# Block 2's first mixer as one stream of steps, with the softmax weights applied by ScalarE

## The reference, cut to what matters

```python
qa, ka, va, qb, kb, vb = jnp.split(hh @ w_in, EVEN_SPLITS, axis=-1)   # 8+2+2 and 8+8+8 heads of 64
qa = rms_norm(qa, a_qn); ka = rms_norm(ka, a_kn); qb = rms_norm(qb, b_qn); kb = rms_norm(kb, b_kn)
qa = rope_2d(qa, row, col); ka = rope_2d(ka, row, col)                 # latents only
# a: 4 query heads share a key head; |q - k| <= 128 among latents, all context keys, and a sink
p = softmax(concatenate([s_loc, s_ctx, s_sink], -1));  o_a = p[..., :nloc] @ vb + p[..., nloc:] @ vc
# b: neighbourhood with a position bias among latents, all context keys, no sink
s_loc = qg @ kg * scale + bias;  s_loc = where(col_ok, s_loc, NEG_INF)
y_lat = concatenate([o_a, o_b], -1) @ w_out                            # y_ctx the same, keys: context only
x = x + g1 * y_lat;  ctx = ctx + cg1 * y_ctx
```

## Time and profile before

| | us |
|---|---|
| Median of 3 timed runs (2628.22 to 2632.52) | 2629.16 |
| The profiled execution's own time | 2625.06 |
| Its span in the profile | 2623.4 |
| TensorE busy | 2340.9 (89%) |
| VectorE busy | 1578.5 (60%) |
| ScalarE busy | 830.6 (32%) |
| Projection of the mixer, from 1273.57 to 1381.10 | 107.53 |
| Head norms, rotation, bias, to 1440.38 | 59.28 |
| Attention, to 1593.50 | 153.12 |
| Output projection, to the first sum of the next norm at 1642.80 | 49.30 |

### The profile page before, as it was taken

The page is one execution under the profiler, slowest core; times in us unless marked ns, Lnnn a source line. Parts: engine busy times, 40 slices in busy tenths (PEclk is TensorE's granted clock), DMA queues, the critical chain, the costliest instruction groups (busy, mean ns, idle before and its releaser), DMA issues.

```text
span 2623.4 us, 39655 instructions
## 1 busy us (share of the span) xinstructions
PE 2340.9 (89%) x14932; PEld 1943.1 (74%) x14932; DVE 1578.5 (60%) x2834; ACT 830.6 (32%) x1274; POOL 29.0 (1%) x58
## 2 busy tenths in 40 slices
PE   8999579999999888999696999599999568797999
PEld 7999448999999877998582557478878453166987
DVE  6666667666666657665535884662552565556764
ACT  4444324444444544443010452011111010153332
POOL 0000000000000000000000000000000000000000
PEclk9999859999999988999896899799999787599999
DMA  7656204665665423666120002022222110001444
GB/s 249 240 208 218 81 0 154 238 213 199 241 230 184 154 97 125 237 221 236 68 96 0 1 1 85 32 96 96 96 96 96 48 65 16 0 1 65 160 169 151
DMA packets 50221, 325.66 MB, mean 124 GB/s; under 512 B 5328, under 2 KB 8656, under 8 KB 16976
## 3 DMA queue, kind: packets, MB, share of 16 engines
q1 hardware_dynamic: 42480, 266.61, 28.9%
q0 software_dynamic: 7648, 57.81, 6.0%
HBM read 323.35 MB, written 1.05 MB: 124 GB/s over the span
## 4 chain that ended last, share of the span: by engine, by line
PE 80%; DVE 14%; ACT 3%; issue 2%; DMA 0%; DVEq 0%; ACTq 0%; PEldq 0%; SPq 0%
PE psum L1319 17%; PE psum L1320 16%; PE psum L1321 16%; PE psum L1406 3%; PE psum L1444 3%; PE psum L1473 3%; PE psum L1407 3%; PE psum L1408 3%; PE psum L1491 3%; PE psum L1465 3%; PE psum L1701 2%; PE psum L1423 2%; PE psum L1480 1%; DVE w_lo L627 1%; PE psum L1702 1%
## 5 line engine op out<-in xcount | busy, mean ns | idle before, releaser
L1319 PE MATMUL psum<-h_hi,w_hi 128*128 128x256 f32 (+2 forms) x2568 | 796.7, 310 | 115.9 <-DVE h_lo L815 84.7
L393 ACT ACTIVATE w_hi<-raw 128x1024 fp32r<-128x1024 f32 (+1 forms) x542 | 513.6, 990 | 859.1 <-PE psum L1321 648.8
L1320 PE MATMUL psum<-h_lo,w_hi 128*128 128x256 f32 (+2 forms) x2568 | 785.1, 306 | 0.0
L1321 PE MATMUL psum<-h_hi,w_lo 128*128 128x256 f32 (+2 forms) x2568 | 784.6, 306 | 0.0
L627 DVE TENSOR_TENSOR w_lo<-raw,w_hi 128x1024 fp32r<-128x1024 f32 (+1 forms) x542 | 599.8, 1148 | 230.9 <-ACT w_hi L393 211.1
L1319 PEld LDWEIGHTS psum<-h_hi,w_hi 128*128 128x128 f32 (+1 forms) x2568 | 496.2, 193 | 162.7 <-issue 64.8
L1321 PEld LDWEIGHTS psum<-h_hi,w_lo 128*128 128x128 f32 (+1 forms) x2568 | 495.9, 193 | 19.4
L1320 PEld LDWEIGHTS psum<-h_lo,w_hi 128*128 128x128 f32 (+1 forms) x2568 | 496.1, 193 | 18.9
L1406 PE MATMUL psum<-g_both,w_hi 128*128 128x256 f32 x704 | 202.4, 287 | 2.1 <-DVE w_lo L627 2.1
L1407 PE MATMUL psum<-g_both,w_hi 128*128 128x256 f32 x704 | 199.1, 283 | 0.0
L1408 PE MATMUL psum<-g_both,w_lo 128*128 128x256 f32 x704 | 199.1, 283 | 0.0
(11 more groups left out here) (231 smaller groups left out, 2888.6 us busy)
## 6 DMA issues: line engine op xcount, KB each, us to landing
raw<-in_weights SPq DMA_DIRECT2D x207, 1024.0 KB, 4.9
raw_ada<-in_ada POOLq DMA_DIRECT2D x48, 1024.0 KB, 6.8
raw<-in_weights SPq DMA_DIRECT2D x64, 704.0 KB, 4.1
arena<-in_rpb POOLq DMA_DIRECT2D x1, 2048.0 KB, 9.7
arena<-in_fox_c POOLq DMA_DIRECT2D x1, 1888.0 KB, 8.7
const_region<-in_even_c POOLq DMA_DIRECT2D x1, 1360.0 KB, 8.8
const_region<-in_latent_c POOLq DMA_DIRECT2D x1, 1296.0 KB, 6.2
x_res<-in_x_lat SPq DMA_DIRECT2D x4, 256.0 KB, 6.9
```

The costliest lines, as they stand in the source:

```text
L393: nc.scalar.activation(wh[s][:, a], raw[s][:, a], ACT.Copy).then_inc(hi_ready, 1)
L1319: mm(out, sh, mh, start=n == 0, stop=False)
L1320: mm(out, sh, ml, start=False, stop=False)
L1321: ins = mm(out, sl, mh, start=False, stop=n == len(pairs) - 1)
```

## The change

Stages 1 to 4 become one list of things to do, `even_order`, which all engines follow. Its items are: a projection unit; the sum of one chunk's squares; a root over the 10 rows of the "a" heads or the 16 rows of the "b" heads; the spread of a chunk; the rotation of a chunk; a "slot" of attention; half an output unit.

The attention's 64 jobs are grouped in 24 steps (`even_steps`): for each kind and each of 4 chunks two wide steps (two heads, one block of 128 queries, 512 keys) and one narrow step (two heads, both query blocks, 256 keys). A slot k has, on TensorE, the scores of step k, the transposes of step k-1 and the value products of step k-2. The two heads of a step lie on partitions 0 to 63 and 64 to 127. Scores of every step use banks 2 and 3, transposes 4 and 5. Slots 0 to 11 (kind a) stand behind projection units 8 to 17 (two slots behind units 12 and 16), slots 12 to 26 behind the projection. Behind slots 15 to 22 stands one half output unit each (12 products, "a" half), and the 8 "b" halves come last.

Other edits: TensorE adds bias and mask as a product with the identity (line 1831 of the kernel after), the factor 1/8 is folded into the query gains, VectorE's maximum takes both heads in one instruction, and the weighting of the exponentials goes from VectorE to ScalarE (a copy with a scale). Squares go from VectorE to ScalarE. The mask is added to the bias by GpSimd in 2 instructions. The key copies go away, since heads c and c+4 form a pair (weights are permuted on the host). In `stick`, the choice of the table set moves behind the square root.

```diff
+            for n in range(18):
+                yield "unit", n
+                if 1 <= n <= 5 or 7 <= n <= 14:
+                    yield "sum", n - 1 - (n > 6)
...
+                if n >= 8:
+                    for _ in range(1 + (n in (12, 16))):
+                        yield "slot", next(slots)
+            for k in slots:
+                yield "slot", k
+                if 15 <= k <= 22:
+                    yield "out", k - 15
+            for q in range(8, 16):
+                yield "out", q
...
+            def step_slot(k):      # ScalarE
+                if k < len(E_STEPS):
+                    s, z = E_STEPS[k], 8 + 4 * (k % 2)
+                    nj = len(s["jobs"])
+                    act.wait_ge(st_shifted, k + 1)
+                    if s["kind"] == "a":
+                        nc.scalar.activation(st_small[:, 32 + z:32 + z + nj], st_small[:, 24 + z:24 + z + nj], ACT.Exp)
+                    for n, (m, t, col) in enumerate(s["jobs"]):
+                        nc.scalar.activation(st_p[:, 2 * (k % 2) + m, col:col + s["L"]], psum[:, 2 + m, col:col + s["L"]],
+                                             ACT.Exp, bias=st_small[:, z + n:z + n + 1],
+                                             accum_out=st_small[:, 8 + z + n:9 + z + n]).then_inc(st_exp, 1)
+                if 1 <= k <= len(E_STEPS):
+                    s, z = E_STEPS[k - 1], 24 + 4 * ((k - 1) % 2)
+                    act.wait_ge(st_rec, k)
+                    for n, (m, t, col) in enumerate(s["jobs"]):
+                        p = st_p[:, 2 * ((k - 1) % 2) + m, col:col + s["L"]]
+                        ins = nc.scalar.activation(p, p, ACT.Copy, scale=st_small[:, z + n:z + n + 1])
+                    ins.then_inc(st_prob, 1)
+                    act.wait_ge(st_turned, k)
+                    wait(act, st_out, k - 2)
+                    for m in range(2):
+                        nc.scalar.activation(st_pt[:, 2 * ((k - 1) % 2) + m, :], psum[:, 4 + m, :],
+                                             ACT.Copy).then_inc(st_turn_in, 1)
...
-                    nc.scalar.preload_act_table_set("natural_log_exp_and_others")
                     for what, k in stick_order():
                         if what == "proj":
                             stage(1, 1, 1, 1, lead=(lambda: square_one(7)) if k == (0, 0) else None)
+                            if k == (0, 0):
+                                nc.scalar.preload_act_table_set("natural_log_exp_and_others")
...
+            def step_shift(k):     # VectorE
+                dve.wait_ge(st_scored, k + 1)
+                ...
+                    step(V.reduce_max(mx, src, AX_X))
+            def step_weigh(k):
+                dve.wait_ge(st_exp, sum(len(v["jobs"]) for v in E_STEPS[0:k + 1]))
+                if s["kind"] == "a":
+                    step(V.tensor_tensor(tot, tot, es, ALU.add))
+                V.reciprocal(rec, tot).then_inc(st_rec, 1)
...
+            def step_scores(k):    # TensorE
+                wait(pe, st_exp, sum(len(v["jobs"]) for v in E_STEPS[0:k]))
+                ...
+                        ins = mm(psum[:, 2 + m, 0:T], ident, bias, start=False, stop=True)
+                ins.then_inc(st_scored, 1)
+            def step_turn(k):
+                pe.wait_ge(st_prob, k + 1)
+                wait(pe, st_turn_in, 2 * k)
...
+            def step_out(k):
+                pe.wait_ge(st_turn_in, 2 * k + 2)
...
+                    elif what == "slot":
+                        if k < len(E_STEPS):
+                            step_scores(k)
+                        if 1 <= k <= len(E_STEPS):
+                            step_turn(k - 1)
+                        if 2 <= k <= len(E_STEPS) + 1:
+                            step_out(k - 2)
```

More of the change, by code:

```diff
@@ new lines, in even_steps @@
+        def even_steps():
+            steps = []
+            for kind in "ab":
+                for c in range(4):
+                    group = 8 * (kind == "b") + 2 * c
+                    for t in range(2):
+                        steps.append(dict(kind=kind, c=c, base=0, L=TJ, jobs=[(m, t, 0) for m in range(2)],
+                                          group=group, first=t == 0, last=t == 1))
+                    steps.append(dict(kind=kind, c=c, base=T, L=T, jobs=[(m, t, t * T) for m in range(2) for t in range(2)],
+                                      group=group + 1, first=True, last=True))
+            return steps
@@ new lines, in even @@
+            def even():
+                sums = 0
+                unit_of = {}
+                for what, k in even_order():
+                    if what == "unit":
+                        if k % 2 == 0:
+                            hi_next(0, 0, 1, pos.e, SLOT)
+                            pos.p += 1
+                        unit_of[k] = pos.u
+                        pos.u += 1
+                        pos.e += 1
+                    elif what == "sum":
+                        act.wait_ge(bank_free, unit_of[k + (k >= 5)] + 3)
+                        wait(act, e_sq_used, sums - 1)
+                        nc.scalar.activation(e_sq[:, sums % 2, :], e_qk[:, k, :], ACT.Square).then_inc(e_sq_made, 1)
+                        sums += 1
+                    elif what == "root":
+                        rows = (10, 16)[k]
+                        act.wait_ge(e_sq_used, (5, 13)[k])
+                        nc.scalar.activation(e_row[0:rows, :], psum[0:rows, 7, :], ACT.Sqrt,
+                                             bias=small[0:rows, 40:41]).then_inc(e_rooted, 1)
+                    elif what in ("spread", "rope"):
+                        pos.u += 1
+                        pos.e += 1
+                    elif what == "slot":
+                        step_slot(k)
+                    else:
+                        if k % 4 == 0:
+                            hi_next(0, 0, 1, pos.e, SLOT)
+                            pos.p += 1
+                        pos.u += 1
+                        pos.e += 1
@@ L562, in _ @@
             norm(TJ)
-            for j in range(9):
-                stage(1, 1, 2, 2)
-            ask(ACT.Sqrt, row_t[0:26, :], row_t[0:26, :])
-            softmax_jobs(list(even_jobs()))
-            stage(2, 2, 2, 4)
+            even()
             norm(TJ)
@@ L1662, in even @@
-                pe.wait_ge(phase_loaded[2], 32)
-                head_norms([(P, TJ)] * 13, 26, TJ, lambda c: e_sel[:, c, 0:26], lambda c, m: e_bsel[0:26, c, :])
-                told()
-                for c in range(5):
-                    b = small_out()
-                    mm(psum[:, b, 0:T], rot_a[:], e_qk[:, c, 0:T], start=True, stop=True).then_inc(small_done, 1)
-                told()
-                softmax_jobs(list(even_jobs()))
-                stage(2, 2, 2, 4, lambda i, j, s: joint_chunks(i, j, s, 2))
+                sums, unit_of = 0, {}
@@ L1946, in _arrays @@
     out["sb_c"] = _join(np.concatenate([m0, m1], axis=1), tri, -np.ones((P, P)))
-    sel, bsel = _head_tables(13, 32)
+    sel, bsel = np.zeros((P, 13, 32), np.float32), np.zeros((32, 13, P), np.float32)
+    for first, n in ((0, 5), (5, 8)):
+        sel[:, first:first + n], bsel[:, first:first + n] = _head_tables(n, 32)
     cos, sin, rot = _rope(P, 16)
```

309 lines of the change are left out of this document (223 added, 86 removed).

## The result

The changed kernel takes 2691.84 us (median of 4 runs, 2688.99 to 2692.62) against 2629.32 for the kernel before (4 runs, 2628.22 to 2632.52): 1.0233 times as long, 95% interval 1.0218 to 1.0248. The forecast was 2702, from a chain of two claims: a stall in every slot, and a clock that falls behind each stall. Both are there.

The account below looks back on a forecast made before the run. TensorE, busy 89% of the span, was taken to bound the kernel: 2625.06 + 24 (mixer at full clock) + 69 (clock) - 20 (`stick`) = 2698, plus 4.1 from profiled execution to median, 2702 us; range 2635 to 2755.

Parts of the forecast that it names:

- Table loads of `stick`: In `stick`, table loads between exponentials and logarithms go: a gain of 20 us, ends 10 and 30.
- TensorE's work in the slots, full clock: In the attention, a pair of heads costs what one head costs: 91 us for what takes 153.12.
- Stall in 24 slots: In every slot, TensorE's transposes wait for ScalarE's weighting, queued behind the next exponentials: 112 us, ends 96 and 127.
- Clock loss in the slots: Behind each of 24 stalls, TensorE's clock falls and loses 2.65 us: 64 us.
- First five spreads, the unit ahead of them left out: In the mixer's norms, the first 5 spreads are not hidden: 5.4 us more than unit 6 itself.
- Mixer in all: The whole changed mixer, 369.2 us before, would be about 440 to 480 us long.
- GpSimd beside VectorE in the norm: In the norm ahead of the mixer, GpSimd's bias and mask addition beside VectorE costs 0 to 4 us, taken as 0.
- Rival 4: In the attention, pairs do not run at once with 512 keys: 41 us on top, 2743 us; chance 0.04.
- the second reciprocal: In the mixer's norms, it stands in front of VectorE's maximum: 2.1 us.
- Rival 1: In the slots, TensorE keeps its clock through the stalls: 69 us go, 2633 us, or 2609 at best; chance 0.13.
- Rival 2: In slots 12 to 26, without full units, the clock stays down: 116 us instead of 69, 2749 us; chance 0.20.
- rival 3: In the slots, transposes find their weights ready: 112 us and most clock loss go, about 2525 us; chance 0.03.

Follow-up runs that it names:

- e6: Kernel before, with only the choice of ScalarE's table set in `stick` moved behind the square root: 2604.77 us, 0.9907 of before.
- e5: Changed kernel with 5 unneeded 512-column products on TensorE between scores and transposes of every slot: 2648.81 us.
- e4: Changed kernel with GpSimd's two additions of mask to bias made to wait for the mixer's first squares: 2687.76 us.
- e3: Changed kernel with 7 unneeded 512-column products on TensorE between scores and transposes of every slot: 2674.04 us.
- e1: Changed kernel with ScalarE's weighting of step k, and VectorE's reciprocal for it, moved from slot k+1 to slot k: 2566.58 us, 0.9764 of before.
- e8: Changed kernel with weighting and reciprocal of step k in slot k, and the weighting on VectorE: 2553.21 us, 0.9717 of before.
- e9: e8 with GpSimd's additions waiting for first squares, VectorE's group reading earlier, second root and reciprocal behind the slot after unit 14: 2550.28 us, 0.9696 of before.
- e7: Changed kernel with the weighting of the exponentials back on VectorE instead of ScalarE, orders else kept: 2650.81 us.

## Why the prediction was right, and where it was off

| Term | forecast | shown |
|---|---|---|
| Table loads of `stick` | -20 | -22.5 in the profiles, -24.3 in e6 |
| TensorE's work in the slots, full clock | 91 | 91.7 (e5: 42.6 + 24.3 + 24.8) |
| Stall in 24 slots | 112 | 110.4: 109.5 in 23 slots, 0.85 in the last |
| Clock loss in the slots | 64 | 51 (e5 against the changed kernel) |
| First five spreads, the unit ahead of them left out | 5.4 | 7.2 (1306.42 to 1313.62) |
| Mixer in all | 462.5 | 449.6 |
| GpSimd beside VectorE in the norm | 0 | +4.4, 4.1 in e4 |
| Same work behind the mixer | 0 | +4.4, from execution to execution |

**The table loads.** Right in size and reason; e6 isolates it. The reason is mainly, but not only, the waits: the two that I had added up to 23.8 us fell to 7.5, and the clock gave about 4 us. By count 17 loads went and none came (23 from 800 us to the norm before, 6 now), where I had one put in.

**Work in the attention.** Right: pairs at once, also with 512 keys. Rival 4 (pairs apart) falls by the row at 1595.61, where four instructions for two heads take 1.06 us.

**The stall.** The deciding step, and right in place, releaser and total. Some of the agreement is luck, since misses cancel. The last stall is 0.85 us, because no scores and exponentials stand ahead of it, and I had counted it at 4.5; the other 23 are 4.76 us on average. The longest, 6.35, holds the second reciprocal, which I had as 2.1 us in a term of its own. And I took 1.15 us for weighting two times 512 and 1.4 for four times 256, and the rows at 720 and 500 ns make it 1.33 to 1.35 and 1.7. Other parts were shorter than I had allowed (the two exponentials 1.34 us from 1599.37 to 1600.71, where I had 1.44), so that the mean of all 24 is 4.60 us where I had 4.67. The trace of before held no such row, and the upper bound (the exponential's 0.72) was the better choice: the copy with its scale took 720 ns, the plain copy out of PSUM 595 (line 581). Both the exponential and this copy read a value per row; no run isolates what that costs.

**The clock.** Right in kind: idle time ahead of the transposes brings it to half, e3 and e5 show it by filling the idle time and changing nothing else. The size was the term most off, 64 for 51, and this is nearly the whole of the 12.9 us by which the mixer was too long in my sum. I had carried one wait's 2.65 us over to all 24. In the changed kernel transposes and values at half clock lose 0.9 + 0.9, and the half unit behind 0.4 to 0.7 (1606.26 to 1609.58 is 3.32 us, the same in e5 2.96), and some steps lost less. Rival 1 (clock holds) falls with PEclk 0.74 to 0.81. Rival 2 (stays down for long, 116 us) falls too: behind each of the eight half output units the scores run at full clock again (1.13 to 1.14 us in the timeline, from 1568.63 to 1664.14), though no full unit stands there. Its case in slots without a unit ahead is seen in part: scores and bias at 1495.42, 1523.44 and 1534.84 take 1.1, 0.8 and 0.2 us more than at full clock.

**The stall hidden** (rival 3, 2525 us). Not in this change, but e1, e8 and e9 are that case, built on purpose: 2567, 2553 and 2550. They stay 42, 28 and 25 us above it, since the 112 us did not all go: in e1 28 us of waits are left, and in e8 20.

**GpSimd.** This step failed: bounded by 0 and 4 and taken at 0, it is 4.4 in the profile, above the bound, and 4.1 in the time. I had looked at where GpSimd's result is needed, and not at what runs on VectorE beside it.

The profiled execution was put at 2698 and is 2691.5: -12.9 for the mixer and -2.5 for `stick`, +4.4 for GpSimd and +4.4 behind the mixer. I had added 4.1 for the distance of the median from the profiled execution before; the changed kernel's median and profiled execution agree within 0.4 us, so that distance belonged to one execution and should not have been carried over.

## What to carry to other kernels

When a pipeline over three engines is given a new order, write out for each engine what stands in front of the instruction for which another engine waits; here work on ready data (the weighting of step k-1) stood behind work on data not yet made (the exponentials of step k), and that cost 110 us of waits and 51 of clock, while the choice of engine cost 13 once the order was mended. Take a composite change apart: one of its edits was worth -24 us. And a wait that is found last in a ring is not the ring: removing its 14 us lowered all waits by 5, and the clock took 4 of these back.

## What the runs showed of the hardware

- Beside GpSimd's addition (two SBUF tensors, 4.58 to 4.60 us an instruction in e4) VectorE's instructions with two tensors in SBUF took longer: the pair of line 927 5.24 us in the changed kernel, where it takes 0.88 in e4, and the pair of `w_lo` 6.25 in e4, where it takes 2.36 in the changed kernel. In each pair nearly all of it falls on one instruction (4.73 us where the others take 0.48, 5.11 where the other takes 1.21), which ends 0.3 us (line 927) or 1.1 us (`w_lo`, at 1274.92) behind the end of GpSimd's second addition. A reciprocal of one tensor (3.35 us at 1227.96 beside it, 3.35 in e4 without it) and a copy out of PSUM (0.69 at 1268.66 beside it in e4, 0.69 at 1263.15 without it) are not stretched. In the trace of before GpSimd makes no addition (its 29.0 us are transfers issued and constants written), so the 0 in the sum was an estimate with no row behind it.
- In the changed kernel ScalarE's copy with one scale per row takes 720 ns for 512 columns and 500 for 256 (line 576); its plain copy of 512 columns out of PSUM takes 595 (line 581).
- The length of a wait alone did not set the granted clock behind it: it was full behind 2.77 and 3.69 us and half behind 2.84 us (e7). Behind those of the eight slots with a half output unit ahead of them in the changed kernel (4.29 to 4.78 us) all transposes ran at half.
- The granted clock fell to 0.50 with no wait, behind four spreads of 16 rows (e5, 1465.32), and to 0.51 where a wait of 1.86 us stood ahead of such spreads (e9, 1408.70). With neither, in e5 from 1538.32 to 1639.00, it was 1.00.
